# Expert stage of a two-layer diffusion step: tiles with a stored hidden product first, tiles that make it in the stage last

## What is computed

```
D_MODEL, PEER_HEADS, PEER_NKEYS, PEER_TOPK = 1024, 8, 128, 16      # 128 * 128 experts

def _peer(x, w_q, sub_keys, u, v):
    ...
    s1, i1 = lax.top_k(s[:, :, 0], PEER_TOPK)
    s2, i2 = lax.top_k(s[:, :, 1], PEER_TOPK)
    cand = (s1[..., :, None] + s2[..., None, :]).reshape(...)
    ...
    best, pos = lax.top_k(cand, PEER_TOPK)
    eidx = jnp.take_along_axis(cidx, pos, axis=-1)
    gate = jax.nn.softmax(best, axis=-1)
    ...
        hb = jax.nn.gelu(jnp.einsum('tkd,td->tk', u[ib], xb), approximate=False)
        return jnp.einsum('tk,tkd->td', gb * hb, v[ib])
```

## Time and profile before

| | |
|---|---|
| median of three runs | 4494.85 us (4488.1 to 4506.34) |
| profiled execution, its own time | 4508.42 us |
| its span, first to last instruction | 4506.9 us |
| busy: TensorE, VectorE, GpSimd, ScalarE | 3912.8, 3036.8, 1631.0, 944.6 us |
| moved by DMA | 1086.11 MB, mean 241 GB/s |
| expert stage of layer 0, first DMA to last output product | 1478.9 to 2401.1 us |
| expert stage of layer 1, likewise | 3577.7 to 4487.5 us |

### The profile page before, as it was taken

One profiled execution on the slowest core, in us unless ns is written; L12 is line 12 of the kernel. 1 busy time (PEld: TensorE's weight loads), 2 busy tenths in 40 slices (PEclk: granted clock), 3 DMA queues, 4 the chain that ended last, 5 costly groups with the idle time before them and its releaser, 6 DMA issues. The chain is left out here.

```text
span 4506.9 us, 51306 instructions
## 1 busy us (share of the span) xinstructions
PE 3912.8 (87%) x17674; PEld 2208.2 (49%) x17674; DVE 3036.8 (67%) x5747; ACT 944.6 (21%) x1311; POOL 1631.0 (36%) x1148
## 2 busy tenths in 40 slices
PE   6999947978688899989998877996868799989998
PEld 2677744644355455544344555563445555434333
DVE  0466662669898677866664675368989777776664
ACT  1211101123355211100002254213336411100000
POOL 0000000027643566655550000005854377665552
PEclk7999968998899999999999899998989999999999
DMA  7111101149799999999991000115879899999996
GB/s 278 49 46 47 36 4 59 57 156 357 262 334 333 330 400 400 390 389 381 391 380 65 28 1 28 47 47 176 269 259 342 317 391 399 401 389 392 382 389 238
DMA packets 391076, 1086.11 MB, mean 241 GB/s; under 512 B 33664, under 2 KB 174208, under 8 KB 384384
## 3 DMA queue, kind: packets, MB, share of 16 engines
q0 software_dynamic: 148480, 539.04, 31.2%
q1 hardware_dynamic: 215936, 463.21, 29.3%
q10 hardware_dynamic: 26496, 81.80, 5.0%
HBM read 998.19 MB, written 85.72 MB: 241 GB/s over the span
## 5 line engine op out<-in xcount | busy, mean ns | idle before, releaser
L1344 PE MATMUL ex_ps_p<-ex_vst_p,ex_gh_p 128*128 128x512 f32 x3072 | 1366.6, 602 | 81.6 <-DMA ex_vst_p<-in_v 81.4
L1344 PEld LDWEIGHTS ex_ps_p<-ex_vst_p,ex_gh_p 128*128 128x128 f32 x3072 | 589.2, 193 | 803.4 <-issue 757.4
L1076 POOL DMA_INDIRECT sp_rows_p<-in_u,sidx_p x512 | 747.2, 1459 | 570.3 <-DVE sp_rows_p L1090 451.6
L1076 POOL DMA_INDIRECT sp_rows_p<-in_v,sidx_p x512 | 657.2, 1284 | 472.4 <-DVE ex_acc_p L1102 350.8
L1090 DVE SCALAR_TENSOR_TENSOR sp_rows_p<-sp_rows_p,xs_p 128x1024 f32<-128x1024 f32 x512 | 648.1, 1306 | 93.5 <-DMA sp_rows_p<-in_u,sidx_p 90.3
L1102 DVE SCALAR_TENSOR_TENSOR ex_acc_p<-sp_rows_p,sp_gsp_p,ex_acc_p 128x1024 f32<-128x1024 f32 x512 | 643.9, 1283 | 44.0 <-DMA sp_rows_p<-in_v,sidx_p 10.1
L755 POOL TENSOR_TENSOR eh_ulo_sl_p<-eh_ust_sl_p,eh_uhi_sl_p 128x1024 bf16<-128x1024 f32 x88 | 208.9, 2374 | 1154.7 <-ACT eh_uhi_sl_p L751 1154.0
L796 PE MATMUL eh_psH_sl_p<-h_hi_p,eh_uhi_sl_p 128*128 128x384 bf16 x704 | 239.9, 341 | 84.9 <-POOL eh_ulo_sl_p L755 83.8
L627 PE MATMUL ps_psA_p<-ps_hT_p,ps_wst_p 128*128 128x128 f32 (+1 forms) x1024 | 287.5, 440 | 16.3 <-ACTq L162 16.3
L354 PE MATMUL rec_psA<-rec_hT,rec_wst 128*128 128x128 f32 (+1 forms) x1024 | 291.5, 436 | 9.0 <-ACTq L162 8.2
L1437 DVE TENSOR_TENSOR ex_gh_p<-ex_est_p,ex_gst_p 128x384 f32<-128x384 f32 x160 | 89.2, 557 | 296.6 <-DMA ex_est_p<-hidden 163.0
(11 more groups left out here) (256 smaller groups left out, 5447.5 us busy)
## 6 DMA issues: line engine op xcount, KB each, us to landing
ex_vst_p<-in_v SPq DMA_DIRECT2D x256, 512.0 KB, 9.9
gates<-gt_gs_p ACTq DMA_DIRECT2D x24, 2048.0 KB, 9.3
ex_ust_p<-in_uT SPq DMA_DIRECT2D x96, 512.0 KB, 7.4
ex_gst_p<-gates SPq DMA_DIRECT2D x64, 768.0 KB, 16.6
eh_ust_sl_p<-in_uT SPq DMA_DIRECT2D x88, 512.0 KB, 4.5
eh_ust_gt_p<-in_uT SPq DMA_DIRECT2D x72, 512.0 KB, 4.4
ex_est_p<-hidden SPq DMA_DIRECT2D x40, 768.0 KB, 19.6
ada_wst<-in_ada_w SPq DMA_DIRECT2D x12, 2048.0 KB, 8.5
```

The source lines that it names most:

```text
L1076: pool.indirect_dma_start(out=self.rows[n % self.NR][:], out_offset=None, in_=src, in_offset=bass.IndirectOffsetOnAxis(ap=self.sidx[:, b, ...
L1344: last = nc.tensor.matmul(psO[b][:, BANK * x:BANK * x + BANK], gh[q][:, P * b:P * b + P], vst[q][:, BANK * x:BANK * x + BANK], start=start ...
```

## The change

The order of the tiles in `peer_experts` is turned round: early tiles come first, late ones last. The early tiles are now the first ones of u (`early_u = uT[:early]`), ET = 4 early groups stand where LT = 4 late groups stood in conditions, and counts that said "late first" say "early first". SyncE now begins with the gates and the stored hidden values of group 0; the first two tiles of u follow, interleaved with v. The tiles of u from the third on are issued from tile ET on. TensorE makes the first products of the first two late tiles inside the last early group. The pace rule keeps its weights, so the three tiles without sparse steps at the end are now late ones.

```
@@ peer_experts
-    LT = J * late
+    ET = J * early
...
-            return 16 * sum(1 if x < late else 2 for x in range(g % 2, g + 1, 2))
+            return 16 * sum(2 if x < early else 1 for x in range(g % 2, g + 1, 2))
...
-            pace = lambda x: 9 * min(x, LT) + 5 * max(0, x - LT)
+            pace = lambda x: 5 * min(x, ET) + 9 * max(0, x - ET)
...
-                sp.dma_start(ust[n % 2][:], uT[n]).then_inc(u_in[n % 2], 16)
+                sp.dma_start(ust[n % 2][:], uT[ET + n]).then_inc(u_in[n % 2], 16)
...
-                if g >= late:
-                    sp.dma_start(est[g % 2][:], hid[J * (g - late):J * (g - late) + J].rearrange("j p t -> p j t")
+                if g < early:
+                    sp.dma_start(est[g % 2][:], hid[J * g:J * g + J].rearrange("j p t -> p j t")
                                  ).then_inc(g_in[g % 2], 16)
 
-            for n in range(2):
-                take_u(n)
             take_gates(0)
             for n in range(NK):
-                if n + 2 < LT:
-                    take_u(n + 2)
+                if n < 2:
+                    take_u(n)
+                if n >= ET and n + 2 < NK:
+                    take_u(n - ET + 2)
                 sp.wait_ge(vp, n + 1)
                 sp.dma_start(vst[n % J][:], v[n]).then_inc(v_in[n % J], 16)
...
-            def group(g, is_early, first=False, last=False):
+            def early_group(g, first=False, last=False):
                 for q in range(J):
-                    if not is_early and not (last and q >= J - 2):
+                    if last and q >= J - 2:
+                        hidden(q - J + 2, q % 2)
+                    output(g, q, start=first and q == 0)
+
+            def late_group(g, last=False):
+                for q in range(J):
+                    if not (last and q >= J - 2):
                         hidden(J * g + q + 2, q % 2)
-                    output(g, q, start=first and q == 0, stop=is_early and last and q == J - 1)
+                    output(g + early, q, stop=last and q == J - 1)
...
-            hidden(0, 0)
-            hidden(1, 1)
-            group(0, False, first=True)
-            with pe.Fori(1, late - 1) as g:
-                group(g, False)
-            group(late - 1, False, last=True)
-            with pe.Fori(late, NG - 1) as g:
-                group(g, True)
-            group(NG - 1, True, last=True)
+            early_group(0, first=True)
+            with pe.Fori(1, early - 1) as g:
+                early_group(g)
+            early_group(early - 1, last=True)
+            with pe.Fori(0, late - 1) as g:
+                late_group(g)
+            late_group(late - 1, last=True)
...
-                act.wait_ge(gr, n + 1)
+                act.wait_ge(gr, ET + n + 1)
...
-            at, turns = 0, [turn_of(b) for b in range(SB)]
+            at, turns = 0, [turn_of(b) - early for b in range(SB)]
             for b in range(SB):
                 if turns[b] < late:
-                    groups(at, turns[b])
-                    at = turns[b]
+                    groups(at, max(at, turns[b]))
+                    at = max(at, turns[b])
                     sparse.gelu(act, b)
...
-                if n >= LT:
+                if n < ET:
                     src = est[g % 2][:, q, :]
                 else:
                     src = ge[n % 2][:]
-                    dve.wait_ge(hg, n + 3)
+                    dve.wait_ge(hg, n - ET + 3)
...
-                if n + 2 < LT:
-                    take_u(n + 2)
+                if n >= ET and n + 2 < NK:
+                    take_u(n - ET + 2)
@@ peer
-    early_u = uT[NK - early:]
+    early_u = uT[:early]
```

## The result

| | before | with the change |
|---|---|---|
| median of the comparison's runs | 4503.09 us | 4517.58 us |
| ratio, 95% interval | | 1.0032 (1.0022 to 1.0041) |
| span of the profiled execution | 4506.9 | 4514.4 |
| expert stage of layer 0 (stage 1), first DMA to last output product | 922.1 | 929.1 |
| expert stage of layer 1 (stage 2), likewise | 909.8 | 915.5 |

A forecast was written before the change was run, and what follows sets the result against it. Early tiles were taken to be bound by transfers, late tiles by PE with transfers close behind. The terms sum to +5.4 and +12.5 us, together +18, which on the median 4494.85 gives 4513 us; range 4482 to 4540.

The forecast's parts named there:

- A: Stage start: PE starts 20.5 us after the stage's first DMA, which costs 13.2 and 14.3 us.
- B: Early tiles, with slightly more row steps each, take 5.81 and 5.97 us; +5.0 and +6.2 us.
- C: Old passage from late to early tiles: its time above pure work goes; -4.9 and -2.1 us.
- D: New passage from early to late tiles: half of two first products fits PE's idle time; -3.9 us per stage.
- E: Early tiles begin with loads landed, worth 0 to 9 us; DVE's later first step takes 4 back; -4 per stage.
- F: Late tiles get slightly more row steps: 0 in stage 1, +2 us in stage 2, between -6 and +5.
- The rival that hid the start wholly: Stage start: transfers go on as they would anyway, no cost beyond the second count; 4510 or a little less; chance 0.20.
- The slower rival: Late tiles with steps become bound by transfers, deciding at over 392 GB/s; +44 us, 4539; chance 0.18.
- the faster rival: Early tiles lose half of their waits, 52 us, at a pace under 5.5; 4461; chance 0.12.
- The second way to count: If transfers bound the whole stage, only its start and end matter; +7.4 us a stage, +15 in all.

The follow-up runs named there:

- Experiment 1: The changed kernel with the first two tiles of u, their low halves and the memsets after the first two groups' gates; ratio to the kernel before 1.0000.
- experiment 4: The changed kernel loading only a quarter of the stored hidden values from the third group on, part of the result left out; ratio to the kernel before 0.9891.
- edits 1 and 2: On the changed kernel: first tiles of u after the first two gates (ratio 1.0000), row steps spread over all 128 tiles (0.9988); both together 0.9972.
- weight 9: The pace rule's 9 kept, row steps over all 128 tiles: new order with edits 1 and 2, ratio 0.9972; old order 0.9956.
- weight 12: 12 in place of 9 in the pace rule, new order with edits 1 and 2; ratio to the kernel before 0.9900.
- experiment 5: Two kernels: the old order with the new order's sharing of row steps, and the new order with the old sharing; ratio to the kernel before 1.0001 each.
- new split (5): The kernel before, in the old order, with the changed kernel's sharing of row steps between early and late tiles; ratio 1.0001.
- weight 10: 10 in place of 9 in the pace rule: new order with edits 1 and 2, ratio 0.9914; old order with row steps over all 128 tiles, 0.9956.
- old split (5): The changed kernel with the old order's sharing of row steps between early and late tiles; ratio to the kernel before 1.0001.
- weight 11: 11 in place of 9 in the pace rule, new order with edits 1 and 2; ratio to the kernel before 0.9892.
- experiment 3: The kernel before, in the old order, with row steps spread over all 128 tiles and not over 125; ratio 0.9956.

## Why the prediction was right

Term by term, forecast against the profiles of before and after, stage 1 and stage 2:

| term | forecast | measured | from |
|---|---|---|---|
| A, start | +13.2, +14.3 | +11.0, +12.2 | first output at T0 + 18.3 and 18.4 |
| B, pace of the early tiles | +5.0, +6.2 | +6.1, +6.7 | 76 x 5.825, 84 x 5.976 |
| C, old change-over | -4.9, -2.1 | -4.9, -2.1 | late tiles end without a wait |
| D, new change-over | -3.9, -3.9 | -2.6, -3.2 | 32.3 us of pure work; four tiles at the pace and three first products would be 34.9 and 35.5 |
| E, full start | -4, -4 | 0, 0 | the pace above has it in already |
| F, late tiles | 0, +2 | 0, -6.2 | 9.05 in both stages |
| not in the sum | | -2.7, -1.8 | three first products at the old start took 14.3 and 13.4 us, not 11.6 |
| sum | +5.4, +12.5 | +6.9, +5.6 | stage lengths +7.0, +5.7 |

**A** had the right chain: the second tile of u, its cast and low half, the memsets, the gate. Experiment 1 took it away and showed that the forecast's full price holds only in part: the start counts by two thirds, and the rest returns as pace. The rival that hid the start wholly fell with it.

**B** was right in both sizes, 5.825 and 5.976 against 5.81 and 5.97, and experiment 4 confirms its ground. The price of a step, 1.4 us by its bytes, holds in the new order: with edits 1 and 2 in both, from weight 9 to weight 12 the pace fell 0.52 us for 0.37 steps in stage 1 and 0.47 for 0.35 in stage 2, about 1.4 and 1.35 each. In the old order, from weight 9 to 10, it was about 1.0 (0.14 us for 0.14 steps, 0.13 for 0.13), and 0.9 and 1.1 for the split of experiment 5; why it is less there was not tried.

**E** did not show. The first group was quick, 22.9 us, but the second took 30.9, and together they are slower than the pace. The full buffers were followed by a stretch in which v came late: PE waited 8.1 us for it in one piece, up to 1532.28, after the hole in the transfers that experiment 1 closed. The 4 us that the forecast took back for the later first step were 1.6 in stage 1: the row steps begin at T0 + 18.3, not T0 + 21.

**F** is the step that failed: "between -6 and +5; +2". It came out at the lower bound. The forecast took steps per tile for bytes per tile: 4.66 steps in place of 4.57, so more to load beside each late tile. But rows are gathered ahead of their tiles, and at the end of the stage there is nothing to gather ahead for. The window of stage 2's 40 late tiles holds 176 gathers and 141.5 MB (362.00 us at 391 GB/s) with the change, and 187 gathers and 145.1 MB (368.20 at 394) before. Over all kernels of the study the length of this window goes by the bytes in it (us times GB/s), whatever the order:

| stage 2, 40 late tiles | MB in the window | us | order |
|---|---|---|---|
| new split (5) | 141.2 | 362.0 | old |
| the change | 141.5 | 362.0 | new |
| weight 9, steps to the end (3) | 143.7 | 362.0 | old |
| weight 10 (7) | 144.4 | 363.7 | new |
| before | 145.1 | 368.2 | old |
| old split (5) | 146.8 | 370.7 | new |
| weight 10 (7) | 147.5 | 372.5 | old |
| weight 11 (7) | 148.9 | 376.0 | new |
| weight 12 (7) | 152.6 | 380.6 | new |

In stage 1 the forecast asked for 398 GB/s, and 384 were drawn. F's miss of 8 us and E's of 8 in the other direction cancelled, so the nearness of the total is in part luck.

The slower rival, transfers taking over the late tiles, did not come to pass here, but it is real: it sets in between 4.7 and 4.9 steps in the new order (9.09 at 4.74, 9.27 at 4.90). By the table, the bytes in the window tell it; the rate does not, and the 392 GB/s that I named was no bound: 397 were drawn over 434 us without a wait, and 394 (before, stage 2) with one. For the faster rival I had read the steps wrong: of the early tiles' steps four of five are dots in stage 1 (152 of 188) and seven of ten in stage 2 (152 of 217), not two of three; it did not come to pass either. The Trainium skill (DMA: Bandwidth & Descriptors, "Where 436 GB/s comes from") gives about 358 GB/s for HBM to SBUF as the share of one of two cores on a stack. The runs say again that this does not bind the one core that this program uses: 401 over 380 us.

The second way to count gave +7.4 a stage and the measured figures are 7.0 and 5.7: of all the workings it came nearest, with two terms in place of six. Its terms fared less well. At the start the row steps begin 1.6 us later in stage 1 (T0 + 18.3 in place of T0 + 16.7), where it had 4 to 5. At the end it set 42.7 us behind the gate of tile 124 against 36.0 before. Stage 1 shows it: that gate comes at 2359.59, 42.0 us before PE's end. Stage 2 does not:

```profile
4460.53 0.55 DVE L1441 TENSOR_TENSOR ex_gh_p<-ex_ge_p,ex_gst_p 128x384 f32<-128x384 f32 x1
```

PE ends at 4495.1, 34.6 us later and 1.4 us less than before. So in stage 2 its nearness, too, is not explained by its terms.

## What to carry to other kernels

Where transfers bound a stage for most of its length, first ask when they stand idle: at the start, while the first consumer waits for something it does not need yet, and at the end. Turning the order of the work round moves these two idle stretches and by itself changed little (0.32%), though with weight 10 the new order was 19 us faster; filling them (steps up to the last tile) and moving bytes from the kind of tile that is bound by them to the kind that is not (the weights) gave 1.1% in the new order, once each kind's own pace had been measured. Count a stretch's bytes by the transfers that fall in it, not by the tiles: what is loaded ahead belongs to the stretch before.

When a sum has several terms of both signs, take the few boundaries of the resource that binds as a check on it. Look at its terms as well, since a near total can come from terms that are off. And compare stages by their lengths: the place where the first expert stage begins moved by 18 us between executions here, more than the whole effect.

## What the runs showed that I had not expected

Steps for the last early tiles cost nothing (experiment 3), though every early tile before the last four is bound by transfers: VectorE is four tiles ahead and has all but three of them behind it when PE begins the last four outputs. And late tiles with the same steps each wait in one order and not in the other. In stage 2 the window's length goes by its bytes in both orders, and fewer fall beside the late tiles when they stand last; in stage 1, with the same bytes, it stays open.
